# Six places for weight units instead of four, with the low parts written over the landed weights

## The reference

```
h = rmsnorm(x, g_mix);  proj = h @ w_in
x = x + (sum over branches of sigmoid(gate) * (y_n @ w_branch[n])) @ w_out
x = x + (act(conv(h2 @ w_up)_gate) * conv(h2 @ w_up)_up) @ w_down
```

## Time and profile before

| | us |
|---|---|
| median of three executions | 1458.99 |
| the profiled execution, device time | 1458.09 |
| its span, first to last instruction | 1456.3 |
| PE busy | 1435.8 |
| PE weight loads busy | 1294.2 |
| POOL busy | 1183.8 |
| ACT busy | 886.1 |
| DVE busy | 660.0 |

### The profile page before, as it was taken

How to read it: one execution, slowest core, us unless ns; L and a number is a source line. 1 busy time by engine, 2 the same in 40 slices (tenths; PEclk the granted TensorE clock), 3 DMA queues, 4 the chain that set the end, 5 groups by cost and what they waited for, 6 DMA issues and landing times.

```text
span 1456.3 us, 29049 instructions
## 1 busy us (share of the span) xinstructions
PE 1435.8 (99%) x9420; PEld 1294.2 (89%) x9420; DVE 660.0 (45%) x1478; ACT 886.1 (61%) x1496; POOL 1183.8 (81%) x926
## 2 busy tenths in 40 slices
PE   8999999999999999999999999999999999999998
PEld 7899998888888899988888889999899999888887
DVE  3653444444445733355444456660563642433333
ACT  5665645766666655647666666866445544655554
POOL 5876686999879876787998979899576899789895
PEclk9999999999999999999999999999999999999999
DMA  7654454666556544454665666556444565566663
GB/s 246 201 159 146 145 160 144 199 193 187 188 178 202 167 153 143 150 178 144 198 190 189 184 212 199 161 176 188 130 145 125 152 189 185 157 190 186 190 188 101
DMA packets 80036, 251.80 MB, mean 173 GB/s; under 512 B 7632, under 2 KB 22480, under 8 KB 79440
## 3 DMA queue, kind: packets, MB, share of 16 engines
q1 hardware_dynamic: 79088, 245.72, 54.3%
q10 hardware_dynamic: 864, 4.92, 0.9%
HBM read 249.56 MB, written 1.05 MB: 172 GB/s over the span
## 4 chain that ended last, share of the span: by engine, by line
PE 93%; DVE 2%; ACT 2%; issue 1%; DMA 1%; POOL 0%; SPq 0%; DVEq 0%; ACTq 0%; POOLq 0%
PE psum L922 20%; PE psum L923 20%; PE psum L924 20%; PE psum L956 18%; PE psum L957 9%; PE psum L1033 1%; PE psum L1021 1%; DMA raw<-in_units 1%; PE psum L1052 1%; PE psum L1043 1%; DVE x L1463 1%; ACT w_hi L428 0%; PE psum L1316 0%; PE psum L1111 0%; PE psum L1352 0%
## 5 line engine op out<-in xcount | busy, mean ns | idle before, releaser
L403 POOL TENSOR_TENSOR w_lo<-raw,w_hi 128x512 fp32r<-128x512 f32 x461 | 602.8, 1308 | 257.2 <-ACT w_hi L428 247.6
L404 POOL TENSOR_TENSOR w_lo<-raw,w_hi 128x512 fp32r<-128x512 f32 x461 | 609.1, 1321 | 0.0
L428 ACT ACTIVATE w_hi<-raw 128x1024 fp32r<-128x1024 f32 x461 | 484.7, 1054 | 92.3 <-PE psum L924 76.6
L956 PE MATMUL psum<-both,w_hi 128*128 128x512 f32 x1088 | 387.6, 399 | 0.0
L922 PE MATMUL psum<-both,w_hi 128*128 128x256 f32 x1192 | 345.4, 290 | 2.3 <-POOL w_lo L404 2.3
L924 PE MATMUL psum<-both,w_hi 128*128 128x256 f32 x1192 | 336.9, 283 | 0.0
L923 PE MATMUL psum<-both,w_lo 128*128 128x256 f32 x1192 | 336.9, 283 | 0.0
L957 PE MATMUL psum<-both,w_lo 128*128 128x256 f32 x1088 | 305.3, 281 | 0.0
L956 PEld LDWEIGHTS psum<-both,w_hi 128*128 128x128 f32 x1088 | 204.3, 188 | 51.2 <-POOL w_lo L404 0.4
L922 PEld LDWEIGHTS psum<-both,w_hi 128*128 128x128 f32 x1192 | 228.0, 191 | 11.8 <-issue 8.6
L923 PEld LDWEIGHTS psum<-both,w_lo 128*128 128x128 f32 x1192 | 228.2, 191 | 0.3
(11 more groups left out here) (276 smaller groups left out, 2118.6 us busy)
## 6 DMA issues: line engine op xcount, KB each, us to landing
raw<-in_units SPq DMA_DIRECT2D x461, 512.0 KB, 3.6
arena<-in_consts ACTq DMA_DIRECT2D x1, 2320.0 KB, 9.4
arena<-in_bias ACTq DMA_DIRECT2D x2, 1024.0 KB, 5.0
arena<-in_consts SPq DMA_DIRECT2D x1, 1657.0 KB, 8.4
out<-arena SPq DMA_DIRECT2D x4, 256.0 KB, 2.6
pre<-in_x SPq DMA_DIRECT2D x2, 256.0 KB, 2.9
arena<-in_x SPq DMA_DIRECT2D x2, 256.0 KB, 4.7
prm<-in_params ACTq DMA_DIRECT2D x2, 153.5 KB, 3.4
```

The lines of the kernel that those rows point to most:

```text
L403: pool.tensor_tensor(w_lo[s][:, 0:D // 2], raw[s][:, 0:D // 2], w_hi[s][:, 0:D // 2].bitcast(F32), ALU.subtract)
L404: pool.tensor_tensor(w_lo[s][:, D // 2:D], raw[s][:, D // 2:D], w_hi[s][:, D // 2:D].bitcast(F32), ALU.subtract)\
L428: act.activation(w_hi[s][:, :], raw[s][:, :], ACT.Copy).then_inc(hi_ready, d.inc(hi_ready))
L956: pe.matmul(bank(4 + k), blocks_of(w_hi[s], c), both[:, 2 * c * T:2 * (c + 1) * T], start=(c == 0), stop=False, skip_group_check=True)
```

## The change

The raw and low buffers now share memory: the names `raw0` to `raw5` are given out in a scope that ends before `w_lo0` to `w_lo5` are made, so that `w_lo[s]` has the address of `raw[s]`. POOL subtracts in place. With the same memory (twelve buffers of 4 KB per partition) there are six places instead of four.

A landing place is now read by TensorE to the end of the unit. So the load of unit u waits for `unit_done` of unit u-6 (nothing for the first six), and no longer for `hi_ready` and `lo_ready`. `high` waits for the landing only, `low` for `hi_ready` only. In layer 1 ACT makes four high parts after the norm instead of three, which puts ACT one unit further ahead at each later place of its program. The constants of line 359 are issued after the sixth load. Loops whose trips hold four units are written out (three in PE's program, one of ACT's helpers), and POOL's and SP's loops take six units a trip.

```diff
+W_RING = 6
-        raw = [sb(f"raw{s}", D) for s in range(RING)]
-        w_hi = [sb(f"w_hi{s}", D, F32R) for s in range(RING)]
-        w_lo = [sb(f"w_lo{s}", D, F32R) for s in range(RING)]
+        raw = []
+        with ExitStack() as landing:
+            for s in range(W_RING):
+                raw.append(landing.enter_context(nc.sbuf_tensor(f"raw{s}", [P, D], F32)))
+        w_lo = [sb(f"w_lo{s}", D, F32R) for s in range(W_RING)]
+        w_hi = [sb(f"w_hi{s}", D, F32R) for s in range(W_RING)]
...
-            for s in range(RING):
-                sp.dma_start(raw[s][:, :], t["units"][s]).then_inc(raw_full[s], d.inc(raw_full[s]))
+            d.skip(unit_done, RING)
+            def landing_free(u):
+                if u is None or u >= W_RING:
+                    sp.wait_ge(unit_done, d.next(unit_done))
...
-            def load(index, s):
-                sp.wait_ge(hi_ready, d.next(hi_ready))
-                sp.wait_ge(lo_ready, d.next(lo_ready))
+            def load(index, s, u=None):
+                landing_free(u)
...
+                for k in range(len(order)):
+                    u = layer * UNITS1 + k
+                    if u == W_RING:
+                        sp.dma_start(arena[:, A1["consts"]:A1["consts"] + NK1], t["consts1"]).then_inc(consts1_full, d.inc(consts1_full))
+                    if RING <= k < UNITS_BEFORE:
+                        load_group(at, k, u % W_RING, u)
+                    else:
+                        load(at + order[k], u % W_RING, u)
...
             def low(s):
-                pool.wait_ge(raw_full[s], d.next(raw_full[s]))
                 pool.wait_ge(hi_ready, d.next(hi_ready))
-                pool.wait_ge(unit_done, d.next(unit_done, 1, "slot"))
                 pool.tensor_tensor(w_lo[s][:, 0:D // 2], raw[s][:, 0:D // 2], w_hi[s][:, 0:D // 2].bitcast(F32), ALU.subtract)
...
                     act.wait_ge(raw_full[s], d.next(raw_full[s]))
-                    act.wait_ge(unit_done, d.next(unit_done, 1, "slot"))
                     act.activation(w_hi[s][:, :], raw[s][:, :], ACT.Copy).then_inc(hi_ready, d.inc(hi_ready))
...
-                norm(load_params1, P1["g_mix"], 2 if layer else 3, True)
+                norm(load_params1, P1["g_mix"], 2 if layer else 4, True)
...
-                with d.loop((CH - 2) // 2) as _:
-                    for _ in range(2):
-                        linear_unit(h_hi, h_lo)
-                        linear_unit(y_hi, y_lo)
+                for _ in range(CH - 2):
+                    linear_unit(h_hi, h_lo)
+                    linear_unit(y_hi, y_lo)
```

More of the change, by code:

```diff
@@ L369, in _ @@
                     else:
-                        load(at + order[u], s)
+                        load(at + order[k], u % W_RING, u)
                 first, end = layer * UNITS1 + len(order), (layer + 1) * UNITS1
-                ahead = -first % RING
-                groups = (end - first - ahead) // RING
-                for u in range(first, first + ahead):
-                    load(u + layer * PAD1, u % RING)
+                groups = (end - first) // W_RING
                 with d.loop(groups) as i:
-                    for s in range(RING):
-                        load(i * RING + (first + ahead + s + layer * PAD1), s)
@@ L379, in _ @@
-                for u in range(first + ahead + groups * RING, end):
-                    load(u + layer * PAD1, u % RING)
-            with d.loop((total_units - REAL) // RING) as i:
-                for s in range(RING):
-                    load(i * RING + (REAL + s + DEPTH * PAD1), s)
-            for u in range(total_units - total_units % RING, total_units):
-                load(u + DEPTH * PAD1, u % RING)
+                    for k in range(W_RING):
+                        load(i * W_RING + (first + k + layer * PAD1), (first + k) % W_RING)
@@ L387, in _ @@
+                for u in range(first + groups * W_RING, end):
+                    load(u + layer * PAD1, u % W_RING)
+            groups = (total_units - REAL) // W_RING
+            with d.loop(groups) as i:
+                for k in range(W_RING):
+                    load(i * W_RING + (REAL + k + DEPTH * PAD1), (REAL + k) % W_RING)
+            for u in range(REAL + groups * W_RING, total_units):
+                load(u + DEPTH * PAD1, u % W_RING)
             for b in range(4):
@@ L405, in low @@
                     .then_inc(lo_ready, d.inc(lo_ready))
-            with d.loop(total_units // RING) as _:
-                for s in range(RING):
+            with d.loop(total_units // W_RING) as _:
+                for s in range(W_RING):
                     low(s)
-            for s in range(total_units % RING):
+            for s in range(total_units % W_RING):
                 low(s)
@@ L783, in gated_branch @@
             def gated_branch():
-                with d.loop(CH // RING * 2) as _:
-                    for k in range(2):
-                        act.activation(chunk(pre, k), slot(take()), ACT.Sigmoid).then_inc(act_out, d.inc(act_out))
-                        high()
-                        d.skip(unit_done)
-                        next_slot()
+                for c in range(CH):
+                    act.activation(chunk(pre, c % 2), slot(take()), ACT.Sigmoid).then_inc(act_out, d.inc(act_out))
+                    high()
+                    d.skip(unit_done)
+                    next_slot()
             for c in range(CH + 2):
@@ L1218, in _ @@
                 linear_unit(h_hi, h_lo)
-            def linear_units(n, src_hi=h_hi, src_lo=h_lo):
-                with d.loop(n // RING) as _:
-                    for _ in range(RING):
-                        linear_unit(src_hi, src_lo)
             def turn_rows(at):
@@ L1409, in _ @@
                     last.then_inc(rbc_ready, d.inc(rbc_ready))
-            with d.loop(3) as _:
-                for _ in range(2):
-                    linear_unit(h_hi, h_lo)
-                    linear_unit(y1_hi, y1_lo)
+            for _ in range(CH - 2):
+                linear_unit(h_hi, h_lo)
+                linear_unit(y1_hi, y1_lo)
             gated_branch()
```

23 lines of the change are left out of this document (7 added, 16 removed).

## The result

The changed kernel takes 1462.68 us, the median of twenty executions, against 1459.00 us for twenty of the kernel before: ratio 1.0023, interval 1.0017 to 1.0030. The forecast was 1459.2 us with a range of 1456.8 to 1462.0, so the median lies above it. A second result is the spread: 1458.85 to 1467.03 us, where the kernel before keeps within 1458.40 to 1459.84 (over all its executions here, those beside the experiments too, within 1457.67 to 1461.94). The profiled execution is the slowest of the twenty, 1467.03 us. So its profile shows the losses at their worst; what is typical is said by the medians alone.

The account below looks back on a forecast made before the run. The prediction took PE to bound the kernel, busy 1435.8 of 1456.3 us (99%). Its terms, +0.6 - 0.5 + 0.1 = +0.2 us, added to the median of 1458.99 gave 1459.2 us, range 1456.8 to 1462.0.

Parts of the forecast that it names:

- Constants issued after load 5 instead of load 7: Value 0: Layer 1's start: PE needs the constants past 39.7 us, they land by 36 even without overlap; 0 us.
- late-landings rival: Late landings hold ACT at three stretches and the last block's constants: slower, 1463 us; chance 0.10.
- Step (d): Layer 2's fifth unit: the high part before the sigmoid waits for its load beside the bias; +0.1 us, ends 0 and +1.
- (c): Layer 1's fifth unit, waiting for slots the second sigmoid frees: sigmoid starts earlier; -0.5 us, ends -0.5 and +2.2.
- PE's busy time moving by more than 2 us: Sign of being wrong: PE's busy time, 1435.8 us in the old profile, itself moves by more than 2 us.
- Step (b): Last attention piece, both layers: ACT's high part waits for a later landing, +0.3 us twice; +0.6, ends +0.4 and +2.5.
- Deeper ring, value 0: Weight pipeline with six places: safer, but PE's one long weight wait stays; 0 us, ends 0 and -3.1.
- the wait at 22.43: PE before unit 1, 2.27 us for POOL's low part: stays, because ACT's order up to that high part is unchanged.
- ACT's waits change their releaser and do not shrink: Before ACT's high parts: 76.6 us of waits for PE become slightly longer waits for DMA.
- In-place subtraction: POOL's low parts: same shapes and instruction, 0 us; POOL may grow from 2.63 to 2.79 us a unit before PE feels it.
- feed-forward loops: All 204 feed-forward units: a high part 0.7 us later fits in ACT's 1.50 us wait before its copy; 0 us.
- written-out loops: Trip ends of three loops: next matmul already starts 0.12 us after the last, so nothing to remove; 0 us.

Follow-up runs that it names:

- three ahead: The changed kernel with ACT making three high parts after layer 1's norm instead of four, constants still early: 1461.84 us.
- late constants and early high part: Two changed kernels, constants after unit 7, unit 1's high part made in the first norm: 1456.08 us (sigmoids moved ahead, three parts after norm) and 1456.70 us (two).
- sigmoids first: The changed kernel, constants early, with two sigmoids in layers 1 and 2 placed ahead of the high parts beside them: 1461.90 us.
- late constants and three ahead: The changed kernel with constants after unit 7 and three high parts after layer 1's norm instead of four: 1459.05 us.
- quarters: The old kernel with unit 1's high part made in the first norm, and POOL's low part in four instructions instead of two: 1478.85 us.
- early high part: The old kernel with unit 1's high part made in ACT's idle time of the first norm, and two after it instead of three: 1455.32 us.

## Why the prediction was wrong

**The step that failed** is "Constants issued after load 5 instead of load 7: Value 0". It asked when the constants themselves are needed (39.7 us, right) and not whom their 1657 KB pass on the way. The parameters of layer 1 never entered the sum: they are issued from ACT's queue at 10.6 us, and eight scalings on ACT and VectorE need them before PE's first unit. Their landing goes from 3.2 us to 5.3 to 5.7 behind six loads, and to as much as 9.2 behind six loads and the constants. Removing the early constants brings 1459.41 us, placing the parameters ahead of them 1459.35, and adding early constants to the old kernel 1461.79. That is shown from three sides. The late-landings rival had the right kind of mechanism, but the place that decides was not in its list; it got 0.10. That its time, 1463, came out so near was luck: it is half of a sum of other places' upper ends.

**Step (d), layer 2's fifth unit**, valued +0.1 with ends 0 and +1: right place, wrong size. In the profiled execution it cost 6.34 - 4.15 = 2.2 us, and another 1.6 at half clock. The step gave no landing time of its own, and (c) took up to 5.0 us beside the bias; here it was 7.0. What decides is open. Layer 2's bias took 4.7 to 5.1 us in the profiles of all five kernels with separate landing and low buffers, and 5.4 to 8.3 us in the nine that work in place: 7.9 in the kernel after, 8.2 with three ahead, but also 7.2 and 8.3 in the two with late constants and early high part. So early constants are not its cause. The parameters-first and the late-constants kernel have the same order of ACT's work, and medians of 1459.35 and 1459.41, which speaks against 3.8 us in most executions.

**No price for half clock.** A lost microsecond of PE was counted as one. With waits of 2 us and more PE was granted 1.2 GHz for 3.4 or 6.8 us in several profiles. A stretch of 3.4 us cost 1.3 to 1.6 us where it stood, of which 0.7 to 0.9 was left at layer 1's fifth unit; the 6.8 us cost 2.3. One sign of being wrong that the prediction named, PE's busy time moving by more than 2 us, did come (+4.5), and this is where it comes from: the late-constants kernel, with full clock, has 1435.7 us.

**The spread.** The forecast took one landing time per transfer. With the same seven transfers in front of them the parameters took 5.7 us in the profile of sigmoids first, 9.2 in the kernel after, and 9.4 with three ahead. Behind late constants they took 5.3 to 5.7 in four profiles. So the size of this step changes between executions. But the parameters-first kernel scatters by 6.1 us too, against 8.2 of the kernel after, 3.1 to 3.5 with late constants and 3.6 of the kernel before in the same set, so their landing is not the only thing that scatters. The slowest executions also have the lowest mean granted clock: 0.996 for the two of the kernel after above 1466 us (0.997 to 0.999 for the other eighteen), 0.997 for the two of the parameters-first kernel above 1462 us (0.998 to 0.999 for the others). So more half clock is a part of it. What sets it off is open, since only one trace of each kernel is kept.

**Step (b), +0.3 twice, did not come.** PE's L1043 near 181 (L1041 after) moved from 181.37 to 185.55, +4.18 against +4.15 at the fifth unit. ACT's high part there shows no wait for a landing; unit loads took a median of 3.3 us, not 3.5. The estimate of 3.2 us from the Trainium skill's page "DMA: Bandwidth & Descriptors", section "Anatomy of one DMA", by which (b) would be 0, came nearer. But that section measured transfers issued by GpSimd, and these are issued by SyncE.

**Step (c)** was right where nothing crowded it: -0.42 for -0.5 in the kernel with late constants. In the kernel after it was +0.46 over unit 1, 0.26 of it the tail of the half clock, within its upper end.

**Deeper ring, value 0.** Right in the medians: with late constants the six places give 1459.41 and 1459.05. The stated reason held too: the wait at 22.43 stays with 2.13 us there. In the kernel after it vanished only because PE came late to it, by 3.85 us at the start of unit 0 and 5.85 at its last matmul. That ACT's waits change their releaser and do not shrink held for four high parts ahead, though 76.6 us for PE became 135.6 us for DMA and not "slightly" more. It is no measure of the time: with late constants such waits are 175.0 us with four ahead (1459.41 us) and 15.5 with three (1459.05 us). Two slips stand in the prediction's working there and change no term. A load lands 3.5 - 2.88 = 0.6 us into the life of unit u-4, which is 0.2 of a unit and not 0.7. And the wait before ended at the end of unit u-4, not at its start.

**In-place subtraction, feed-forward loops, written-out loops: 0.** All right. A half takes 1.311 us, PE shows no new wait in the feed-forward loops, the loops alone measure 1.0000. The prediction read the Trainium skill's page "Runtime: NRT & Kernel Launch", section "Instruction fetch mechanics", as saying that they would gain. That section speaks only of a branch whose target lies outside the fetched window of two blocks of 256 instructions. A trip of these loops has 202 recorded instructions of PE in the trace, so by this estimate the target may lie inside, and the run does not test the rule.

**Not foreseen at all:** the phase between POOL's halves and DVE's operations near 1180, a wait of 0.6 us in the kernel after, of 0.9 us with late constants and three ahead, none there with late constants and four ahead. It changes with the weights' stream, so it can probably turn out in one's favour as well; no run shows that.

## What to carry to other kernels

When a large transfer is moved earlier, don't ask when it is needed but who is issued behind it on any queue and how soon that one is needed; the smallest transfer can be on the critical path, and issuing it first cost nothing here. Before buying depth for a pipeline, look whether the stall that is to be removed is one of landing or one of order: here one high part moved into an idle microsecond of ACT brought 3.7 us, and six places brought none. A buffer that is shared over its whole life needs a landing and both conversions within the time of the other places, so count these before giving up separate ones.

## What the runs showed of the hardware

- **The clock at a wait.** PE went to 0.50 of full clock at waits of 4.2 us (kernel after) and 4.4 us (three ahead), at one of 5.2 us (quarters, 911.24 to 918.07, begun within the wait), and at some of 2.0 to 2.3 us. The length of a short wait doesn't decide: the wait of 2.27 us before unit 1 has it with loops written out and with parameters first, and hasn't in the kernel before; the wait of 2.12 or 2.13 us has it in the old kernel with early constants and with sigmoids first, and hasn't in the two late-constants kernels. The four kernels with the early high part wait less than 1 us before units 0 and 1, and had no slow stretch there. What decides at some 2 us stays open.
- **A small transfer behind large ones.** 153.5 KB issued on another queue took 2.7 to 3.2 us with four units issued before it, 6.8 with four and the constants, 5.3 to 5.7 with six, and 5.7, 9.2 and 9.4 with six and the constants. The other queue did not shield it.
- **DVE held by GpSimd.** 0.42 us becomes up to 1.5 us for a 128x256 operation with two operands in SBUF, and its excess follows the length of POOL's instruction (median 1.51 with halves of 1.31 us, 0.96 with quarters of 0.76).
- **A fixed part of GpSimd's time.** 128x512 takes 1.31 us, 128x256 takes 0.76.
